# Paired modulation tiles at the start, and split products for a key and value projection, in a two-block fp32 model on one core

## The reference

```python
cs = jax.nn.silu(c)
mod = cs @ mod_w[l] + mod_b[l]           # six vectors of 1024: shift, scale, gate, twice
h = rmsnorm(x, norm_mix[0]) * (1 + sc_m) + sh_m
u = h @ w_in                              # 1024 -> 2 * 1280: y branch and x branch
xc = causal_conv4(u[..., 1280:]) + conv_b
g = blockwise(xc) @ w_gates               # then sigmoids and a linear recurrence over time
x = x + g_m * ((scan(...) * gelu(u[..., :1280])) @ w_out)
x = x + g_f * swiglu(modulate(rmsnorm(x, norm_ffn[0])), w_gate, w_up, w_down)
kv = modulate(rmsnorm(x, kv_norm), kv_shift, kv_scale) @ w_kv   # 1024 -> 512 keys, 512 values
```

## Time and profile before

| | |
|---|---|
| three runs | 2212.54, 2213.38, 2213.91 us (median 2213.38) |
| the profiled execution, its own time | 2211.93 us |
| its span | 2210.1 us, so 1.8 us lie around it |
| busy: TensorE, VectorE, ScalarE | 2181.8, 1541.2, 1169.5 us |
| DMA over the span | 428.19 MB, mean 194 GB/s |

### The profile page before, as it was taken

How to read it: one execution, slowest core, us unless ns; L and a number is a source line. 1 busy time by engine, 2 the same in 40 slices (tenths; PEclk the granted TensorE clock), 3 DMA queues, 4 the chain that set the end, 5 groups by cost and what they waited for, 6 DMA issues and landing times.

```text
span 2210.1 us, 40739 instructions
## 1 busy us (share of the span) xinstructions
PE 2181.8 (99%) x17030; PEld 2129.5 (96%) x17030; DVE 1541.2 (70%) x2570; ACT 1169.5 (53%) x1950; POOL 2.1 (0%) x6
## 2 busy tenths in 40 slices
PE   7999999999999999999999999999999999999999
PEld 6889998999999999999999999999999999999998
DVE  6868996776578688755655865596879656657663
ACT  3645453554544567445644644454766456546443
POOL 0000000000000000000000000000000000000000
PEclk9999999999999999999999999999999999999999
DMA  9959996366655554444454555555654544454553
GB/s 369 337 185 371 372 373 239 126 227 212 191 181 166 184 187 155 152 153 138 121 163 161 174 173 165 169 191 183 198 167 146 179 125 134 150 185 172 186 177 115
DMA packets 123190, 428.19 MB, mean 194 GB/s; under 512 B 14528, under 2 KB 18816, under 8 KB 122368
## 3 DMA queue, kind: packets, MB, share of 16 engines
q1 hardware_dynamic: 123008, 425.58, 58.2%
HBM read 422.87 MB, written 2.66 MB: 193 GB/s over the span
## 4 chain that ended last, share of the span: by engine, by line
PE 91%; DVE 4%; DMA 2%; ACT 1%; issue 0%; SPq 0%; ACTq 0%
PE stream L505 26%; PE stream L507 26%; PE stream L506 26%; PE stream L521 4%; PE side L701 2%; PE side L708 1%; DVE w_lo L421 1%; DMA mod_raw<-in_mod_w 1%; DMA x_res<-in_x 1%; DVE mod_raw L1469 1%; PE side L517 1%; PE side L512 1%; PE side L513 1%; PE stream L512 0%; PE side L630 0%; PE side L842 0%
## 5 line engine op out<-in xcount | busy, mean ns | idle before, releaser
L505 PE MATMUL stream<-h_hi,w_hi 128*128 128x272 f32 (+1 forms) x3280 | 945.1, 288 | 0.0
L507 PE MATMUL stream<-h_hi,w_lo 128*128 128x272 f32 (+1 forms) x3280 | 936.9, 286 | 0.0
L506 PE MATMUL stream<-h_lo,w_hi 128*128 128x272 f32 (+1 forms) x3280 | 934.4, 285 | 0.0
L421 DVE TENSOR_TENSOR w_lo<-raw,w_hi 128x1024 fp32r<-128x1024 f32 (+1 forms) x642 | 769.1, 1205 | 148.7 <-ACT w_hi L970 147.4
L970 ACT CAST w_hi<-raw 128x1024 fp32r<-128x1024 f32 (+1 forms) x642 | 654.2, 1035 | 249.8 <-DMA raw<-in_ffn_down 83.9
L505 PEld LDWEIGHTS stream<-h_hi,w_hi 128*128 128x128 f32 x3280 | 618.8, 189 | 1.7
L507 PEld LDWEIGHTS stream<-h_hi,w_lo 128*128 128x128 f32 x3280 | 619.0, 189 | 0.0
L506 PEld LDWEIGHTS stream<-h_lo,w_hi 128*128 128x128 f32 x3280 | 617.9, 188 | 0.5
L505 PE MATMUL stream<-f_hi,w_hi 128*128 128x256 f32 (+1 forms) x704 | 199.0, 283 | 0.0
L507 PE MATMUL stream<-f_hi,w_lo 128*128 128x256 f32 (+1 forms) x704 | 198.7, 282 | 0.0
L506 PE MATMUL stream<-f_lo,w_hi 128*128 128x256 f32 (+1 forms) x704 | 198.2, 282 | 0.0
(11 more groups left out here) (389 smaller groups left out, 3045.9 us busy)
## 6 DMA issues: line engine op xcount, KB each, us to landing
raw<-in_ffn_up SPq DMA_DIRECT2D x176, 512.0 KB, 3.9
mod_raw<-in_mod_w SPq DMA_DIRECT2D x96, 512.0 KB, 5.6
raw<-in_ffn_down SPq DMA_DIRECT2D x64, 512.0 KB, 3.6
raw<-in_a_cx SPq DMA_DIRECT2D x32, 512.0 KB, 4.1
raw<-in_up_a SPq DMA_DIRECT2D x32, 512.0 KB, 3.5
raw<-in_up_b SPq DMA_DIRECT2D x32, 512.0 KB, 3.5
raw<-in_b_kq SPq DMA_DIRECT2D x32, 512.0 KB, 3.5
raw<-in_up_c SPq DMA_DIRECT2D x32, 512.0 KB, 3.5
```

What stands on the lines that cost most here:

```text
L421: eng.tensor_tensor(w_lo[:, x.slot, 0:x.kb * P], raw[:, x.slot, 0:x.kb * P], w_hi[:, x.slot, 0:x.kb * P].bitcast(F32), ALU.subtract).then_ ...
L505: pe.matmul(ps, w_hi[:, x.slot, W], rhs[0][:, k, off:off + n], start=first, stop=False)
L506: pe.matmul(ps, w_hi[:, x.slot, W], rhs[1][:, k, off:off + n], start=False, stop=False)
L507: return pe.matmul(ps, w_lo[:, x.slot, W], rhs[0][:, k, off:off + n], start=False, stop=last)
```

## The change

- The first 16 modulation tiles come as pairs (scale tile k, shift tile k), x behind the first tile, and `lru_x` chunks 0 to 3 between the pairs. VectorE makes scale and shift column by column, the softplus block behind the fourth pair. ScalarE does squares, root and softplus before the input tiles. `lru_x` has lead 4 and waits for input tile k at step k. The filler products come after the sum.
- Modulation tiles: `lru_x` 4 (10 before), `lru_gates` 6 (8), `lru_y` 8 (6), `lru_out` 8 (4), mostly on its first chunks, `ffn_up0` 38 (36), `ffn_down0` 24 (16 and 4 late), `kv_v` 0 (4).
- `kv_k` and `kv_v` are no longer plain: weights are split as elsewhere, and the input is split into `h_hi` and `h_lo`; `raw_low` now makes the low half for `kv` too.
- The sum of squares comes at step 9 of the first group (7 before). The heads inside `attn_out` stand at k = 1, 3, 5, 6 (1, 3, 4, 5). The last transposition of a value phase follows the second tile of the next phase (the first, before).

```diff
@@ -38,7 +38,7 @@
-FIRST_MODS = tuple(range(DT8, 2 * DT8)) + tuple(range(DT8))
+FIRST_MODS = tuple(m for k in range(DT8) for m in (DT8 + k, k))
@@ -126,14 +126,14 @@
-    ph = [Phase("lru_x", "conv_split", 10, mods=10, **mix),
-          Phase("lru_gates", "gates", 10, "XC", (4,), mods=8, plain=True, **seq),
-          Phase("lru_y", "act", 10, mods=6, **mix),
-          Phase("lru_out", "resid", 8, "XC", (5, 5), norm="ffn0", mods=4, plain=True, **seq),
-          Phase("ffn_up0", "glu", 44, lead=4, mods=36, quiet=8, raw=4, raw_of="ffn0", raw_rhs="RA", **seq),
-          Phase("ffn_down0", "resid", 8, "F", (8, 8, 6), norm="kv", mods=16, late=4, **seq),
-          Phase("kv_k", "act", 4, lead=4, raw=4, raw_of="kv", raw_rhs="HX", plain=True, **seq),
-          Phase("kv_v", "vtok", 4, mods=4, raw=4, raw_of="kv", raw_rhs="HX", plain=True, **seq),
+    ph = [Phase("lru_x", "conv_split", 10, mods=4, lead=4, **mix),
+          Phase("lru_gates", "gates", 10, "XC", (4,), mods=6, plain=True, **seq),
+          Phase("lru_y", "act", 10, mods=8, **mix),
+          Phase("lru_out", "resid", 8, "XC", (5, 5), norm="ffn0", mods=8, plain=True, **seq),
+          Phase("ffn_up0", "glu", 44, lead=4, mods=38, quiet=8, raw=4, raw_of="ffn0", raw_rhs="RA", **seq),
+          Phase("ffn_down0", "resid", 8, "F", (8, 8, 6), norm="kv", mods=24, **seq),
+          Phase("kv_k", "act", 4, lead=4, raw=4, raw_of="kv", raw_rhs="H", **seq),
+          Phase("kv_v", "vtok", 4, raw=4, raw_of="kv", raw_rhs="H", **seq),
@@ -182,11 +182,14 @@
-        if p.name == "lru_y":
-            m -= 2
+        if p.name == "lru_out":
+            p.mods_at = [2, 2, 1, 1] + [0] * 5 + [1, 0, 1] + [0] * (len(p.seq) - 12)
+            assert sum(p.mods_at) == p.mods
+    assert sum(sum(p.mods_at) for p in ph[:3]) + 6 >= 3 * DT8
@@ -377,9 +380,8 @@
-            if n != "kv":
-                low_first[n] = low_at + (n in SHIFT or n == "pre0")
-                low_at = low_first[n] + DT8
+            low_first[n] = low_at + (n in SHIFT or n == "pre0")
+            low_at = low_first[n] + DT8
@@ -445,15 +447,20 @@
-            for m in FIRST_MODS[:DT8 + 2]:
-                load_first(m)
+            load_first(FIRST_MODS[0])
-            for m in FIRST_MODS[DT8 + 2:]:
-                load_first(m)
+            load_first(FIRST_MODS[1])
+            lead = by["lru_x"].lead
+            for k in range(1, DT8):
+                if k <= lead:
+                    load(*chunks_all[k - 1])
+                load_first(FIRST_MODS[2 * k])
+                load_first(FIRST_MODS[2 * k + 1])
-                load(p, x)
+                if x.g >= lead:
+                    load(p, x)
@@ -555,10 +562,10 @@
-                            if not seen[1]:
-                                seen[1] = 1
-                                pe.wait_ge(side["x_in"], DT8)
-                                pe.wait_ge(side["x_shift"], 1)
+                            if k + 1 > seen[1]:
+                                seen[1] = k + 1
+                                pe.wait_ge(side["x_in"], k + 1)
+                                pe.wait_ge(side["x_shift"], k + 1)
@@ -690,7 +697,7 @@
-                    inside={1: lambda: head(7), 3: lambda: head(8), 4: lambda: head(9), 5: lambda: head(10)})
+                    inside={1: lambda: head(7), 3: lambda: head(8), 5: lambda: head(9), 6: lambda: head(10)})
@@ -876,17 +883,18 @@
-                            inside = {7: lambda: sum_up(p.raw_of, p.T if p.raw_of in SHIFT else SEQ)}
+                            inside = {9: lambda: sum_up(p.raw_of, p.T if p.raw_of in SHIFT else SEQ)}
+                    if i == 1 and last_turn:
+                        turn(by[last_turn], by[last_turn].n - 1)
-                        for t in (2, 1):
-                            turn(by[last_turn], by[last_turn].n - t)
+                        turn(by[last_turn], by[last_turn].n - 2)
@@ -921,11 +929,11 @@
-            keep_busy(8)
+            keep_busy(8)
@@ -1383,14 +1391,14 @@
-            act.wait_ge(side["x_scale"], 1)
-            for k in range(DT8):
-                act.activation(HX[:, k, META:], X[:, k, META:], ACT.Identity, scale=col(SM, GS + k)).then_inc(side["x_in"], 1)
+            for k in range(DT8):
+                act.wait_ge(side["x_scale"], k + 1)
+                act.activation(HX[:, k, META:], X[:, k, META:], ACT.Identity, scale=col(SM, GS + k)).then_inc(side["x_in"], 1)
@@ -1704,8 +1712,9 @@
-                        for t in (2, 1):
-                            take_values(by[last_turn], by[last_turn].n - t)
+                        take_values(by[last_turn], by[last_turn].n - 2)
+                    if last_turn and x is p.seq[1]:
+                        take_values(by[last_turn], by[last_turn].n - 1)
@@ -2061,25 +2070,34 @@
-            for m in FIRST_MODS[:DT8]:
-                mod_tile(m)
+            c, g = SHIFT["mix0"] + 8, PCOL["norm_mix"]
-            mod_section(1, 1, DT8)
-            c, g = SHIFT["mix0"] + 8, PCOL["norm_mix"]
-            stt(SM[:, GS:GS + 8], MOD[:, c:c + 8], 1.0, PV[:, g:g + 8], ALU.add, ALU.mult).then_inc(side["x_scale"], 1)
-            for m in FIRST_MODS[DT8:]:
-                mod_tile(m)
-            dve.wait_ge(mod_done, MOD_FIRST)
-            tt(HX[:, :, META - 2:META], MACC[:, 0:8].unsqueeze(2).to_broadcast([P, DT8, 2]),
-               MOD[:, 0:8].unsqueeze(2).to_broadcast([P, DT8, 2]), ALU.add).then_inc(side["x_shift"], 1)
-            sp = SM[:, SPW + 30:SPW + 40]
-            one_plus(SM[:, SPW:SPW + 10], SM[:, SPW + 10:SPW + 20], 1)
-            softplus(SM[:, SPT:SPT + LT], SM[:, SPW:SPW + 10], SM[:, SPW + 20:SPW + 30], SM[:, SPW + 10:SPW + 20],
-                     sp, SM[:, DTT:DTT + LT], SM[:, DTT + 16:DTT + 16 + LT], 1)
-            ts(SM[:, SPL:SPL + LT], SM[:, DTT + 16:DTT + 16 + LT], -8.0, None, ALU.mult)
-            ts(SM[:, SPL2:SPL2 + LT], SM[:, DTT + 16:DTT + 16 + LT], -16.0, None, ALU.mult)
-            own.wait(ts(SM[:, SPT:SPT + LT], SM[:, DTT + 16:DTT + 16 + LT], 8.0, None, ALU.mult))
+            own.wait(ts(MOD[:, c:c + 8], MOD[:, c:c + 8], 1.0, None, ALU.add))
+            def scale_in(k):
+                dve.wait_ge(mod_done, 2 * k + 1)
+                stt(col(SM, GS + k), col(MACC, c + k), col(MOD, c + k), col(PV, g + k), ALU.add, ALU.mult).then_inc(side["x_scale"], 1)
+            def shift_in(k):
+                dve.wait_ge(mod_done, 2 * k + 2)
+                tt(HX[:, k, META - 2:META], col(MACC, k).to_broadcast([P, 2]), col(MOD, k).to_broadcast([P, 2]), ALU.add)\
+                    .then_inc(side["x_shift"], 1)
+            for k in range(DT8):
+                mod_tile(FIRST_MODS[2 * k])
+                if k:
+                    shift_in(k - 1)
+                mod_tile(FIRST_MODS[2 * k + 1])
+                scale_in(k)
+                if k == 3:
+                    sp = SM[:, SPW + 30:SPW + 40]
+                    one_plus(SM[:, SPW:SPW + 10], SM[:, SPW + 10:SPW + 20], 1)
+                    softplus(SM[:, SPT:SPT + LT], SM[:, SPW:SPW + 10], SM[:, SPW + 20:SPW + 30], SM[:, SPW + 10:SPW + 20],
+                             sp, SM[:, DTT:DTT + LT], SM[:, DTT + 16:DTT + 16 + LT], 1)
+                    ts(SM[:, SPL:SPL + LT], SM[:, DTT + 16:DTT + 16 + LT], -8.0, None, ALU.mult)
+                    ts(SM[:, SPL2:SPL2 + LT], SM[:, DTT + 16:DTT + 16 + LT], -16.0, None, ALU.mult)
+                    own.wait(ts(SM[:, SPT:SPT + LT], SM[:, DTT + 16:DTT + 16 + LT], 8.0, None, ALU.mult))
+            shift_in(DT8 - 1)
```

## The result

The changed kernel takes 2227.06 us (median of four runs, 2225.97 to 2229.31), the kernel before 2213.57: a ratio of 1.0066, 95% interval 1.0053 to 1.008. It is 13.5 us slower; 2209.7 was forecast, and 2218 was the top of the range. Its profiled execution took 2227.43 us with a span of 2225.6, which is 15.5 more than the span of before.

A forecast was written before the change was run, and what follows sets the result against it. TensorE, busy 99% of the span, was taken as the bound, so only its passes and waits count. -6.0 - 4.9 - 1.1 + 8.3 = -3.7 gave 2208.2 us profiled, 2209.7 median; range 2202 to 2218, the forecast's own 2206 to 2214.

The forecast's parts named there:

- e: ffn_down0: extra VectorE work, 16.9 us against 12.2 idle, makes TensorE wait 4.3, plus 4 from a loop: 8.3 us more.
- c: Waits at the last kv_v transposition (1.7 us) and the sum (1.2) go; 1.8 comes at the first kv_v transposition.
- b: kv_k and kv_v: 64 products, each 0.077 us shorter as three split ones than plain: 4.9 us less.
- a: Start through lru_out: lead of four lets lru_x begin near 24.7, and lru_out begin 6.0 us earlier; bounds 3 to 7.
- d: Moved waits, summed with c to -1.1 us; attn_out head steps, split transpositions and bank order were to give nothing.
- The loop: ffn_down0: SyncE's tile issue waits for VectorE, the next weight chunk queues behind; 4 us taken, between 0 and 13.
- seven single lacks: Upper bound in e: seven places with doubled modulation tiles, each short by up to 1.8 us, 13 in all.
- The slower one: Rival: the loop bites at every doubled place, ffn_up0 too; e is 17.3, total +5.3, 2218.7 us; chance 0.13.
- The start's rival: Rival: slow first passes or the softplus block leave the start only -3; total -0.7, 2212.7 us; chance 0.15.
- The Trainium skill's fit: Transfer estimate of 3.2 us for 512 KB; the loop would then cost nothing, the sum 4 us lower; loaded rows disagreed.

The follow-up runs named there:

- before_kv3: The kernel before with only the kv_k and kv_v products split in three instead of plain: 2217.62 us, 1.0025.
- before_moved: The kernel before with only the modulation tiles of ffn_down0 and kv_v placed as in the changed kernel: 2213.97 us, 1.0007.
- plain_moved: The changed kernel with only the kv products plain again, modulation tiles left moved: 2213.33 us, 1.0005.
- pool_mods: The changed kernel with modulation tiles from ffn_down0 on issued by GpSimd's queue instead of SyncE's: 2217.64 us, 1.0023.
- pool_high_first: The changed kernel with GpSimd issuing modulation tiles from ffn_down0 on, and ScalarE making h_hi before its waiting cast in ffn_down0: 2216.32 us, 1.002.
- high_first: The changed kernel with ScalarE, in ffn_down0, making h_hi ahead of the cast that waits for a transfer: 2223.38 us, 1.0044.

## Why the prediction was wrong, step by step

Most of the miss is in one step, e. By the ledger of the two profiled executions the change costs 15.5 us where -3.7 was summed, 19.2 more; 13.8 of them are e (22.1 us for 8.3), 2.2 the transposition in c, 1.9 the start with `ffn_up0`, 0.8 the passes of b, 0.5 the rest.

- **a, start, -6.0: held.** `lru_x` starts at 25.86 (24.7 forecast), ends at 60.7 (59.8), `lru_gates` waits 1.2 and 1.3 us (3), there is no wait before `lru_out`, and the stage ends 5.2 us earlier (6.0). Alone, with the sum and turn of c, the start gives 6.5 us. `ffn_up0` gave back 1.1, which had not been counted, so that 4.1 us are left of it where `ffn_down0` begins. Two rows of TensorE's timeline, to hold against the earlier trace rows, and the two waits in the gates:

```profile
20.90 3.62 PE L658 MATMUL side<-params,ones 128*128 128x256 f32 x16
25.86 1.11 PE L528 MATMUL stream<-h_raw,raw 128*128 128x258 f32 x4 [1.34 <-ACT h_raw L1401]
```

```profile
67.69 1.97 PE L528 MATMUL stream<-xc,raw 128*128 128x256 f32 x8 [1.22 <-DVE conv_out L1675]
70.98 1.32 PE L528 MATMUL stream<-xc,raw 128*128 128x256 f32 x5 [1.32 <-issue]
```

- **b, three products, -4.9: the size of the passes held, their price did not.** Kv took 32.4 us, of which 5.3 are waits and 2.6 the lower clock (28 passes); what is left, 24.5, is 4.1 below before's 28.6. But b was summed as TensorE's time alone. The rest of the cost, casts and subtractions that put ScalarE's and VectorE's blocks of work in front of TensorE in kv, had only a 1.8 us guess in c and 2.3 us of work in e. In `before_kv3` the waits from kv to the first heads are 9.7 us and not 1.7, and the kernel has +5.2 where -4.9 stood. This step failed on its own, whatever the tiles do.
- **c, d, -1.1: held in parts.** The 1.7 and the 1.2 went. The new wait at the first `kv_v` transposition is 2.9 (1.8 taken, 0 to 4), and 1.1 us of passes at the lower clock follow it.
- **e, VectorE, 8.3: failed, in size and in kind.** The stage lost 18.2 us, and 2.4 and 1.5 more where kv begins (wait and clock). The 4.3 of it were worked out as an overload of VectorE; yet VectorE was idle for 16.9 us. The loop was named, with SyncE's order as its middle, but as seven single lacks of 1.2 to 1.8 us with a top of 13 (the prediction's own places, four and two, are six, so its top was 10.8). Three things were missing: the `h_lo` was counted as 3.2 us of work "with the wait for ScalarE's first", and not as a wait, five times, on a cast six chunks ahead, with the low weights, the tile and so the next transfer queued behind it (10.5 us); a turn that comes late makes the next late, so the lacks do not stay single (opening the turn at SyncE took the waits for `h_hi` away as well); and a stop of TensorE was followed by passes at the lower clock, 3.9 us in this stage. With plain kv the prediction's terms would leave 11.4 us of work against 12.2 idle, so only the loop's 4 us; `before_moved` has 3.9 in the stage and `plain_moved` 6.7, so without the link the loop was sized about right. The waits also begin earlier than the last third of the stage (at 311.45, with the stage from 277.3 to 357.8).
- **The rivals.** The slower one had the right sign (2218.7, chance 0.13), but its condition, the loop at every doubled place, does not hold in `ffn_up0`, where TensorE waits 0.2 us; and it lacks 8.4 us. It was not right by its mechanism. The start's rival (a = -3) is out.
- **The page.** The Trainium skill's fit for one transfer ("DMA: Bandwidth & Descriptors", "Anatomy of one DMA", 3.2 us for 512 KB, an estimate by that page) was weighed in the prediction and set aside; the trace after has 4.9 and 5.8 us in this stage, and where GpSimd issues the tiles, as on that page, `pool_mods` has a median of 7.7 us, so the loaded stage still does not agree.

Open: whether the last 4 us in `pool_high_first` are bytes or VectorE; why moved tiles cost 1.5 us with the old start and 7.1 with the new one (TensorE is 4 to 5 us nearer to the transfers, which is argued and not shown); why `high_first` gains so much less over the whole than in the stage; and the 1.1 us in `ffn_up0`. A fifth buffer in the ring would test the loop directly, but did not fit in SBUF and was not tried.

## What to carry to other kernels

When an edit adds a short step to an in-order engine, price not its length but what it waits for, and what stands behind it: here a 0.4 us `h_lo` waited for a cast that waited for a transfer, and the issue of the next transfer stood two steps behind it. Price parts of a change in pairs as well: +1.5 and +5.2 made +12.9. And read the stage behind as well when a cure shortens one: here up to 2.6 us only moved on into kv. A faster product that needs casts from engines which were free of it is a gain only if their queues are empty ahead of it at that point.

## What was not expected of the hardware

After some waits of 2 to 3 us TensorE's passes of 256 columns went from 0.118 to 0.213 us apart, for 12 to 15 passes, starting 0.7 to 1.3 us after it resumed (319.69, 339.63) or at once (351.29); after the waits of 2.85 us at 311.45 and 1.40 us at 328.38 they did not. And the DMA engines moved 381 to 391 GB/s over the whole stage in three of these kernels, with the column at 1.00 or 1.01, against 362 GB/s at 0.97 before. A column of 1.00 is no ceiling of the bytes either: the start in the earlier trace rows has 420 GB/s at 1.03.
